# The expert stage of a two-block transformer kernel, rebuilt: split fp32r products, 8 KB weight runs, one fixed slot per expert, row lists made by a product

## The reference, cut to what matters

```python
def hier_moe(h, rg_w, rg_b, re_w, re_b, w_gate, w_up, w_down):
    gp = softmax(h @ rg_w + rg_b);  g_w, g_idx = top_k(gp, 1)          # 4 groups
    el = (h @ re_w + re_b) of the chosen group                          # 8 experts in each
    e_w, e_idx = top_k(softmax(el), 2);  e_w = g_w * e_w / sum(e_w)
    for e in range(32):                                                 # comb: weights by token and expert
        he = silu(h @ w_gate[e]) * (h @ w_up[e])                        # 1024 -> 256, twice
        y = y + comb[:, e:e + 1] * (he @ w_down[e])                     # 256 -> 1024
```

## Time and profile before

| what | value |
|---|---|
| median of three runs | 3032.42 us (3030.88 to 3032.81) |
| the profiled execution's own time and span | 3032.6 us, the same for both |
| PE, DVE, ACT, POOL busy over the span | 89%, 35%, 26%, 26% |
| expert loop, first to last row turn | 575.6 to 978.0 us |
| scatters `d_y<-y_out` (one per slot) | 36 |
| HBM read and written | 298.68 MB, 22.66 MB |

### The profile page before, as it was taken

The page is one execution under the profiler, slowest core; times in us unless marked ns, Lnnn a source line. Parts: engine busy times, 40 slices in busy tenths (PEclk is TensorE's granted clock), DMA queues, the critical chain, the costliest instruction groups (busy, mean ns, idle before and its releaser), DMA issues.

```text
span 3032.6 us, 29962 instructions
## 1 busy us (share of the span) xinstructions
PE 2690.8 (89%) x11350; PEld 2001.2 (66%) x11350; DVE 1069.4 (35%) x1664; ACT 795.4 (26%) x1438; POOL 803.2 (26%) x337
## 2 busy tenths in 40 slices
PE   6997987499999499999999579999888899899997
PEld 4675666233333379887889557888765666688886
DVE  3294453221211323332342434242312435342423
ACT  2333322000000323334333323222222323332222
POOL 2331122211212032223222313444422110134443
PEclk9898787699999799999999579999978878699999
DMA  4421022488888221121211312323221100123331
GB/s 142 135 69 42 28 92 84 167 296 300 302 279 293 86 84 56 56 70 56 70 56 56 113 42 83 97 89 92 83 64 56 54 30 14 34 81 94 97 97 69
DMA packets 277015, 311.82 MB, mean 103 GB/s; under 512 B 24752, under 2 KB 215824, under 8 KB 276912
## 3 DMA queue, kind: packets, MB, share of 16 engines
q1 hardware_dynamic: 262736, 297.65, 29.9%
q0 software_dynamic: 7648, 12.70, 1.2%
q10 hardware_dynamic: 6528, 0.03, 0.1%
HBM read 298.68 MB, written 22.66 MB: 106 GB/s over the span
## 4 chain that ended last, share of the span: by engine, by line
issue 53%; PE 16%; POOL 11%; DVE 1%; ACT 0%; DMA 0%; POOLq 0%; SPq 0%; DVEq 0%; ACTq 0%
POOL w_low L2327 10%; PE bank L1004 9%; PE bank L1017 4%; PE bank L985 1%; PE bank L1129 1%; PE bank L1107 0%; PE bank L664 0%; PE bank L666 0%; PE bank L665 0%; PE bank L990 0%; POOL og L2409 0%; DMA xg<-d_rows,gather_rows 0%; PE bank L1116 0%; DVE xn L1762 0%; PE bank L698 0%
## 5 line engine op out<-in xcount | busy, mean ns | idle before, releaser
L2327 POOL TENSOR_TENSOR w_low<-raw,w_high 128x2048 fp32r<-128x2048 f32 x149 | 683.7, 4590 | 1750.1 <-ACT w_high L1328 1750.1
L664 PE MATMUL bank<-h_high,w_high 128*128 128x512 f32 x1120 | 453.1, 405 | 17.6 <-DVE h_low L1742 7.8
L665 PE MATMUL bank<-h_low,w_high 128*128 128x512 f32 x1120 | 446.0, 398 | 0.0
L666 PE MATMUL bank<-h_high,w_low 128*128 128x512 f32 x1120 | 444.7, 397 | 0.0
L664 PE MATMUL bank<-w_high,h_high 128*128 128x512 f32 (+1 forms) x832 | 345.7, 416 | 29.8 <-POOL w_low L2327 25.6
L1328 ACT ACTIVATE w_high<-raw 128x2048 fp32r<-128x2048 f32 x149 | 284.5, 1910 | 330.7 <-PE bank L666 330.4
L665 PE MATMUL bank<-w_low,h_high 128*128 128x512 f32 (+1 forms) x832 | 331.6, 399 | 0.0
L666 PE MATMUL bank<-w_high,h_low 128*128 128x512 f32 (+1 forms) x832 | 330.8, 398 | 0.0
L1004 PE MATMUL bank<-m_w,xt 128*64 128x512 f32 x576 | 264.0, 601 | 0.0
L664 PEld LDWEIGHTS bank<-h_high,w_high 128*128 128x128 f32 x1120 | 216.8, 194 | 69.5 <-DVE h_low L1742 10.3
L666 PEld LDWEIGHTS bank<-h_high,w_low 128*128 128x128 f32 x1120 | 216.3, 193 | 46.7
(11 more groups left out here) (297 smaller groups left out, 3201.1 us busy)
## 6 DMA issues: line engine op xcount, KB each, us to landing
raw<-in_ffn_w_gu SPq DMA_DIRECT2D x88, 512.0 KB, 4.5
m_w<-in_w_gate SPq DMA_DIRECT2D x74, 512.0 KB, 5.5
m_w<-in_w_up SPq DMA_DIRECT2D x74, 512.0 KB, 6.3
raw<-in_a_w_in SPq DMA_DIRECT2D x72, 512.0 KB, 4.6
m_w<-in_w_down SPq DMA_DIRECT2D x36, 1024.0 KB, 8.5
raw<-in_ffn_w_down SPq DMA_DIRECT2D x40, 512.0 KB, 4.6
raw<-in_w_in SPq DMA_DIRECT2D x34, 512.0 KB, 4.4
raw<-in_b_w_in SPq DMA_DIRECT2D x24, 512.0 KB, 4.5
```

The costliest lines, as they stand in the source:

```text
L664: pe.matmul(out, sta[0], mov[0], start=start, stop=False)
L665: pe.matmul(out, sta[0], mov[1], start=False, stop=False)
L666: return pe.matmul(out, sta[1], mov[0], start=False, stop=stop)
L2327: pool.tensor_tensor(out=w_low[:, slot, :], in0=raw[:, slot, :], in1=w_high[:, slot, :].bitcast(F32), op=ALU.subtract).then_inc(low_done, 1)
```

## The change

**Weights.** Gate and up are now loaded with eight consecutive matrix rows per partition, one 8 KB run per partition and matrix (`(p k) n`). The width of the model is permuted to match: `norm_tile(..., turned=True)` writes `xn` with a stride, and the router's weights are loaded in the same order. ACT writes the fp32r high half of gate and up (`up_high`) and DVE the low half (`up_low`), each in two pieces of 128x2048 per slot. The rows get both halves side by side as 128 stationary columns (`xt[..., 0:R]` high by ACT, `R:2R` low by DVE), and gate and up become 16 fp32r products into 128 rows of a bank. ACT copies rows 64 to 127 out (`lower`), and DVE adds them to rows 0 to 63 (`gated`, in two halves) before silu and the product.

**Slots.** Slot e < 32 is always expert e; slots from 32 on are further tiles. Slots 0, 1 and 2 have known experts, and their weights are loaded before the router has run: slot 0 (into `w_first`) and gate and up of slot 1 once phase 3 has read the gates, slot 2 after phase 4. ACT and DVE split slot 0 during phase 5.

**Row lists.** `d_list`, its 8 indirect DMAs and its load are gone. DVE builds one-hot matrices of row and slot, and PE multiplies them (8 fp32 products) into `slot_rows`.

**Moved.** The splits of `B_DIL` and `B_DIL + 1` go behind the expert loop on ACT and POOL, and the load of `B_DIL + 1` behind the loads of `y_in`.

```diff
 # SP
+        sp.wait_ge(pj_low, 8)
+        gate(w_first, 0, m_first); up(w_first, 0, m_first); down(w_first, 0, m_first)
+        gate(w_ring[1], 1, m_up[1][0]); up(w_ring[1], 1, m_up[1][1])
...
+        def next_up(j, b):
+            e = slot_of(j)
+            sp.wait_ge(m_low, 2 * j - 3)
+            gate(w_ring[b], e, m_up[b][0])
+            sp.wait_ge(m_low, 2 * j - 2)
+            up(w_ring[b], e, m_up[b][1])
+        def next_down(j, b):
+            e = slot_of(j)
+            sp.wait_ge(m_down, j - 1)
+            down(w_ring[b], e, m_dn[b])
...
+        with sp.Fori(2, n_less) as i:
+            next_down(2 * i - 1, 1); next_up(2 * i + 1, 1)
+            next_down(2 * i, 0);     next_up(2 * i + 2, 0)
...
+        load_wide(B_DIL + 1, a["a_w_in_2"][0], 4, 0)         # after the y_in loads
 # PE: up(j, b, before); rows_come, turn_rows, down as before
             pe.wait_ge(m_xt, j + 1)
+            pe.wait_ge(m_high, 2 * j + 2)
+            for k in range(KD):
+                if k == KD - 1 and before is not None:
+                    pe.wait_ge(m_he, before + 1)
+                pe.matmul(G[b][:, :], xt[:, b, k, :], up_high[:, b, k, :], start=(k == 0), stop=False)
+            if before is not None:
+                turn_he()
+            pe.wait_ge(m_low, 2 * j + 2)
+            for k in range(KD):
+                last = pe.matmul(G[b][:, :], xt[:, b, k, :], up_low[:, b, k, :], start=False, stop=(k == KD - 1))
 # ACT
+        def gate(j, b):
+            act.wait_ge(m_gu, j + 1)
+            act.activation(lower[:, :], G[b][R:2 * R, :], ACT.Copy).then_inc(m_lower, 1)
+            act.wait_ge(m_gated, 2 * j + 1)
+            act.activation(sg[:, :], gated[:, 0:FE], ACT.Silu).then_inc(m_silu, 1)
+        def period(j, b, uses):
+            gate(j - 1, 1 - b)
+            up_next(j + 1, 1 - b, uses, 0)                    # high half of gate, 128x2048
+            rows_high(j + 1, 1 - b)
+            turned_he(j - 1)
+            up_next(j + 1, 1 - b, uses, 1)                    # high half of up, 128x2048
 # DVE
+        def up_part(ring, b, q):
+            dve.tensor_tensor(out=up_low[...], in0=ring[:, q, :], in1=up_high[...].bitcast(F32),
+                              op=ALU.subtract).then_inc(m_low, 1)
+        def period(j, b, i=None):
+            inner(j - 1, 1 - b)
+            if i is not None:
+                out(j - 2, b, i)
+            up_next(j + 1, 1 - b, 0)
+            rows(j + 1, 1 - b)
+            up_next(j + 1, 1 - b, 1)
 # POOL: step(j, b) as before
+        split_low(B_DIL, B_DIL % 2)                           # after the last scatter
+        split_low(B_DIL + 1, (B_DIL + 1) % 2)
```

More of the change, by code:

```diff
@@ L191, in two_blocks_kernel @@
[L191 to L200, removed]
+    g_wide = at("g_wide", 93, [P, D])
+    rt_raw = at("rt_raw", AR + 76, [P, KD, 36])
+    rt_split = at("rt_split", AR + 77.25, [P, KD, 72], F32R)
@@ L551, in up @@
[L551 to L564, removed]
@@ L566, in _ @@
-        sp.dma_start(gw1[:, :], a["final_norm_g"].partition_broadcast(P)).then_inc(gw1_loaded, 16)
[L567 to L577, removed]
+        sp.wait_ge(wo_out, 8)
+        gate(w_ring[0], 2, m_up[0][0])
@@ L971, in _ @@
         last.then_inc(rt_cum, 1)
+        pe.wait_ge(rt_hot, 1)
+        for c in range(2 * NT):
+            last = pe.matmul(SB[0][0:R, 0:SLOTS], row_hot[:, c, :], slot_hot[:, c, :], start=(c == 0), stop=(c == 2 * NT - 1))
+        last.then_inc(rt_list, 1)
         phase_end(5)
@@ L1041, in _ @@
         down(2 * n_trips - 1, 1, n_trips)
-        for q in range(2):
-            pe.wait_ge(m_up[0][q], 32 * n_trips + 32)
-            last = pe.matmul(SB[1][0:R, 0:R], ident[:, 0:R], m_w[:, 0, q, 0:R], start=True, stop=True)
         phase_end(6)
@@ new lines, in period @@
+        def period(j, b, uses):
[4 more added lines that the diff above has]
+            up_next(j + 1, 1 - b, uses, 1)
+        rows_high(0, 0)
+        rows_high(1, 1)
+        period(1, 1, 1)
+        with act.Fori(1, n_less) as i:
+            period(2 * i, 0, i + 1)
+            period(2 * i + 1, 1, i + 1)
+        period(2 * n_less2 + 2, 0, n_less2 + 2)
+        gate(2 * n_less2 + 2, 0)
+        turned_he(2 * n_less2 + 2)
@@ L1543, in _ @@
+        gate(2 * n_less2 + 3, 1)
+        turned_he(2 * n_less2 + 3)
         phase_end(6)
+        split_high(B_DIL, B_DIL % 2, B_DIL // 2 + 1)
+        split_high(B_DIL + 1, (B_DIL + 1) % 2, (B_DIL + 1) // 2 + 1)
         for i, (second, t) in enumerate(TWO_NORMS):
@@ L2024, in _ @@
         step(sub(starts, ends, ntile[:, :]))
-        begin, cut = rv[:, 0:2, :], rv[:, 3:5, :]
+        slots = cst[:, C_SLOT:C_SLOT + NE]
+        step(dve.scalar_tensor_tensor(out=starts, in0=starts, scalar=float(NE - 1), in1=slots,
+                                      op0=ALU.add, op1=ALU.subtract))
+        over, cut, own = rv[:, 0:2, :], rv[:, 3:5, :], rv[:, 6:8, :]
         for k in range(2):
@@ L2041, in _ @@
-        dve.tensor_copy(pos[:, :], posf[:, :, :].rearrange("p k t -> p (k t)")).then_inc(rt_pos, 1)
-        step(dve.tensor_tensor(out=slotf[:, :, :], in0=ends[0:1, :].unsqueeze(1).broadcast_to([1, SLOTS, NE]),
-                               in1=cst[0:1, C_SLOT:C_SLOT + SLOTS].unsqueeze(2).broadcast_to([1, SLOTS, NE]),
+        step(add(posf[:, :, :], own, over))
+        step(add(posf[:, :, :], posf[:, :, :], cut))
+        dve.wait_ge(vec_loaded, 16 * 8)
+        step(dve.tensor_scalar(id_less[:, :], ids[:, :], float(-OOB), None, ALU.add))
@@ L2045, in _ @@
+        step(dve.tensor_tensor(out=slotf[:, :, :], in0=ends[0:1, :].unsqueeze(1).broadcast_to([1, SLOTS - NE, NE]),
+                               in1=cst[0:1, C_SLOT:C_SLOT + SLOTS - NE].unsqueeze(2).broadcast_to([1, SLOTS - NE, NE]),
                                op=ALU.is_le))
[L2046 removed]
+        dve.wait_ge(rt_list, 1)
+        dve.tensor_scalar(slot_rows[:, :], SB[0][0:R, 0:SLOTS], float(OOB), None, ALU.add).then_inc(rt_slots, 1)
+        dve.tensor_copy(slote[:, 0:NE], cst[0:1, C_SLOT:C_SLOT + NE])
```

325 lines of the change are left out of this document (199 added, 126 removed).

## The result

The changed kernel takes 3094.09 us, median of 4 runs (3092.59 to 3103.33), the kernel before 3031.65 on the same chip (3030.05 to 3032.81). The ratio is 1.0205, 95% interval 1.0187 to 1.0224. The forecast was 3052 with a range up to 3088, so the direction was right and the size was not.

What follows compares the result with a forecast made beforehand. PE bound the kernel's loop (11.49 us a slot), and afterwards the scatter-gather chain stretched by DVE holding POOL would: 3032.6 - 18.7 + 27.5 + 11 = 3052.4, forecast 3052 us, 8-in-10 range 2972 to 3088.

Steps and rivals of the forecast that it cites:

- before the loop: Up to the end of the first down: earlier phase 5, row list and weights, -18.7 us, bounds -10 and -24.
- loop, 34 periods: Expert loop: period 12.3 us in place of 11.49 over 34 periods, +27.5 us; period bounds 11.5 and 13.4.
- last down to PE's turn: After the loop: B_DIL + 1 waits behind y_in, +7.7 at the first square, with POOL's part +11, bounds +3 and +13.
- Each sign that I had named: In the loop: period near 12.3, POOL copies about 2 us, last down product waiting for xg, PE clock below 1.0.
- The rival of 8.9 us: Expert loop: the gather's chain does not bind, DMA and PE bind at 8.9 us; total 2937, chance 0.15.
- the landing: Expert loop: time from the issue of the gather's DMA until its rows arrive, taken as 3.4 to 4.8 us.
- D: End of one slot's down in the expert loop, the zero point of the period walked through.
- The slot of the second kind: Loop slot with PE starting at 1.2 GHz: POOL's gather copy slips in, DMA issued at 6.5, slot 11.5 to 12.2 us.
- that of the first kind: Loop slot at full clock: both POOL copies held, gather issued at 8.3 to 8.6, slot 12.6 to 14.3, say 12.8 us.
- the chain: Expert loop: down's end, y_out copies, scatter, gather, landing, last down product; 10.3 us however fast PE is.
- The hold-up: Expert loop: DVE's two subtractions with two SBUF inputs make POOL's copies and indirect DMAs wait; period 12.3 us.
- The first rival: Expert loop: POOL is not held up, the chain binds at 10.35 us; total 2986, chance 0.22.

Runs made afterwards that it cites:

- e11: Changed kernel with e1, e7 and e5's order of loads on SP together: 2927.5 us, ratio 0.966 to the kernel before.
- e14: e11 with DVE's subtractions in the four pieces of e9: 2926.3 us, ratio 0.965 to the kernel before.
- e2: Changed kernel, DVE's two subtractions per slot reading their second input from PSUM (wrong low halves), order kept: 3091.5 us.
- e4: Changed kernel with half of the gate and up weights loaded in the loop (2.1 MB a slot, wrong result): 3042.4 us.
- e5: Changed kernel with the gate and up loads ahead of the down load on SP: 3100.9 us.
- e3: Changed kernel with the edits of e1 and e2 together (wrong low halves): 2937.5 us.
- e9: On top of e1 and e7, DVE's 128x2048 subtractions in four pieces of 128x512: 2932.8 us.
- e10: Changed kernel with four unused fp32 products on PE ahead of the wait for xg, to keep its clock up: 3088.6 us.
- e7: On top of e1, ACT splits weight block B_DIL + 1 after five of the eight norms behind the loop: 2939.1 us.
- e1: Changed kernel with POOL's scatter one step later, behind the gather of slot j+2: 2949.8 us, ratio 0.972 to the kernel before.

## Why the prediction was right in direction and short in size

By its own terms, in the profiled execution (the measured time from the copy of `y_out` in one slot to that in another; "last down" is slot 35's):

```
term                     forecast   measured
before the loop            -18.7      -11.9   first y_out copy 586.52 against 598.38
loop, 34 periods           +27.5      +67.9   13.49 against 11.49
last down to PE's turn     +11        +10.9   44.74 against 33.84
rest of the program          0         +1.8
sum                        +19.8      +68.7
```

- **Mechanism of the loop: right in its steps, wrong in what ends last.** Each sign that I had named is there: copies of 2.07 us in lines 2488 and 2481, a wait for `xg` in nearly all slots, a clock below 1.0, slots of two kinds (11 and 20 of 31, and not in turn). That PE's 3.1 us, the extra loads and the two roundings would not decide was right too. The rival of 8.9 us did not come true in this order, and is what e11 and e14 reach (8.67).
- **The step that failed is the landing.** I wrote that the gather lands 3.4 to 4.8 us after its issue and that "the lower end is likelier, as the slot's 3.15 MB, issued at D, are through by then". They are not: the last of them lands 11.9 us after D by the mean, and the last product starts at 12.1 where the copy was held and at 12.4 where it was free. The slot of the second kind, put at 11.5 to 12.2, took 13.55 for that reason, and that of the first kind, put at 12.8, took 13.71. e2, e4 and e5 show it from three sides.
- **The rate that I had would not have been enough.** The prediction has 3.38 MB in 8.8 to 9.8 us, and used that for a period of its own. It belongs in the chain, where it begins at D, because the down load on SP waits for the end of a down and the gate and up loads stand behind it. But by it the weights would be there at 9.8 at the latest, and the gather of the first kind, issued at 8.3, would still have landed near 11.7. Measured are 10.9 to 13.4. In the slot from 839.6 us the DMA engines moved 198 GB/s in the first 3.2 us after the down load's issue, 363 in the next 5.0 and 281 in the last 3.0, against the 346 to 382 that I had taken. Why the burst is slower is not shown.
- **The hold-up, on which the argument spent most, was priced wrong by this.** As a mechanism it is shown (e2, e3, e9). As a term of this order it is 0.24 us a slot between two profiled executions, not the 2 between 10.35 and 12.3. The first rival's 2986 for "POOL is not held up" was tried in e2: 3091.
- **A pause costs at its end too.** After the longer pauses of PE the last product of down and the next turn run at 1.2 GHz (1.97 us in place of 1.07 in 11 of 31 slots, 1.11 in place of 0.71 in 16 of 34 turns). I had counted the low clock only for the gate and up products. e10 puts the net of all of it at 0.25 us a slot.
- **Before the loop**, -18.7 against -11.9. Of the 6.8 missing, 3.7 stand in the profile before 70 us, in a stage that the change does not touch. The granted clock there is 0.95 from 36 to 70 us against 1.00 before. The 14 other runs with the same early code are 0.3 to 3.2 us late at the same product of PE, so part of it belongs to this execution, which is also 9 us above the median; how much is the program's is open. 2.8 are the strided write of `xn`, 1.96 to 2.07 us against 1.28, for which I had named 2 and taken nothing. The list came 1.9 sooner after phase 5 began than I had it (50.9 us against 52.8), and the first slot took 3.1 longer. From its first up (569.66) to the turn behind its down (585.24) are 15.6 us against the 13.7 between my two times, and then its `y_out` copy waits 1.2 more for DVE, which does the next slot's two adds and product first. What lies between the steps makes up the rest.
- **After the loop**, the size was right: the block behind `y_in` was waited for and cost 9.5 us at the first square (forecast 7.7) and 10.9 with POOL's part (forecast 11). e7 gives 4.6 of it back.
- **Which work of POOL is held.** The Trainium skill ("SBUF — State Buffer", section "Who interferes with whom") says that copies are excluded and infers that descriptor generation is not. By the runs the copies are (2.07 us), and so are indirect DMAs: 0.95 us by the median, 2.1 to 2.9 in 27 of the 74 of e1, and none over 1.2 in e3, where the second input comes from PSUM. The measurement decides: an indirect DMA on POOL is held too, and the 1.91 us of the earlier trace rows fits. An indirect DMA also reads its row numbers from SBUF, and no run here tells whether that reading or the generation of descriptors is held. In the changed kernel the two met only twice, both times by the start of the loop (2.2 us), so it moved next to nothing there.

What stays open: why the 3.15 MB take 10.9 to 13.4 us from D, and from which bytes in flight a gather is delayed, as only 3.15 and 2.1 MB a slot were tried. The kernel before had the DMA engines busy 84% too, and its gathers landed after 4.8 us by the median.

## What to carry to other kernels

Where a small transfer closes a loop, look up what large ones are issued just before it from the same event. Here it landed when they had landed, and an issue 2 to 4 us earlier bought next to nothing. Two delays that end at the same point hide each other, so taking away one at a time may show little; take away both, or give the wait a period of slack. Here the faster PE brought nothing until the chain of one period was moved, and that was one shift of one step in one queue.

## What the runs showed of the hardware that was not expected

- The same gather lands 2.0 us after its issue in the last two slots of the changed kernel, where no gate and up weights are in flight. In the slots from 613 us to there it takes 3.2 to 5.3 us (issued 8.3 us after the end of the down, where the slot's 3.15 MB start), 4.8 to 7.4 (issued at 6.4) or 6.8 to 8.9 (issued at 4.4, e2, from 600 to 900 us).
- DVE with two inputs in SBUF holds POOL's 64x1 copy until its own end (2.07 us for a copy of 0.18), with one input in PSUM and the same 2.27 us not at all; with four operations of 0.69 us in a row POOL gets in between.
- The same hold lengthens an indirect DMA on POOL from 0.95 to as much as 3.0 us (e7; 2.9 in e1).
- DVE's 128x1024 operation that writes its output with a stride of 128 elements takes 1.96 to 2.07 us against 1.28; PE's turn of 64x128 with a stride of 8 elements 0.136 us against 0.089 at full clock (1.09 and 0.71 for eight).
